# Moving a depthwise convolution from VectorE and GpSimd to TensorE, with half-size adaLN loads, in a two-layer hybrid attention and convolution backbone

## The reference

```python
for l in range(DEPTH):                        # DEPTH = 2
    mod   = silu(c) @ w_ada[l] + b_ada[l]     # six 1024-wide vectors (shift, scale, gate) x 2
    mod_c = silu(c_ctx) @ w_ada[l] + b_ada[l] # the same for the context
    h = modulate(rmsnorm(x, g_mix[l]), sh1, sc1)
    q, k, v, u = split_in(h @ w_in[l])        # 8 query heads, 2 key/value heads, u: 2 x 512
    a_out  = latent_attention(rope(q), rope(k), v, k_ctx, v_ctx, sink)
    cv_out = conv_module(u, ...)
    x = x + gt1 * merge_groups(a_out, cv_out, ...)   # rmsnorm of each, then @ w_out
    x = x + gt2 * swiglu(modulate(rmsnorm(x, g_ffn[l]), sh2, sc2))   # d_ff = 2816

def conv_module(u, w_dw, b_dw, ln_g, ln_b):   # w_dw: 31 taps x 512 channels
    z = u[..., :512] * sigmoid(u[..., 512:])
    z = depthwise_conv(z, w_dw, pad 15) + b_dw       # along the tokens, channel by channel
    return silu(layernorm(z, ln_g, ln_b))
```

## Time and profile before

| | |
|---|---|
| median of 3 runs | 1822.05 us (1820.49 to 1824.18) |
| profiled execution, first to last instruction | 1815.9 us |
| so outside the span, taken from the median | 6.15 us |
| PE busy | 1543.5 us (85%) |
| DVE busy | 1074.1 us (59%) |
| ACT busy | 630.1 us (35%) |
| POOL busy | 523.2 us (29%) |
| chain of work that ended last | PE 59%, DVE 25% of the span |
| HBM read | 146.71 MB |

### The profile page before, as it was taken

How to read it: one execution, slowest core, us unless ns; L and a number is a source line. 1 busy time by engine, 2 the same in 40 slices (tenths; PEclk the granted TensorE clock), 3 DMA queues, 4 the chain that set the end, 5 groups by cost and what they waited for, 6 DMA issues and landing times.

```text
span 1815.9 us, 24713 instructions
## 1 busy us (share of the span) xinstructions
PE 1543.5 (85%) x9388; PEld 1320.2 (73%) x9388; DVE 1074.1 (59%) x1612; ACT 630.1 (35%) x1002; POOL 523.2 (29%) x374
## 2 busy tenths in 40 slices
PE   4976636759889999999999999655778899999997
PEld 1765426647678887888788879654656898998995
DVE  2599999978644332334224356998877644444445
ACT  2310117984343411222112233114974453222222
POOL 0399999803300000000000003999913100000000
PEclk8988767989899999999999999877988999999998
DMA  8332300001111233213332252111001222223222
GB/s 346 115 127 97 135 24 12 1 1 36 39 55 58 89 138 134 68 58 104 141 114 59 95 206 70 47 35 35 1 1 58 82 92 93 92 88 92 93 84 84
DMA packets 35929, 149.80 MB, mean 82 GB/s; under 512 B 3984, under 2 KB 4368, under 8 KB 29712
## 3 DMA queue, kind: packets, MB, share of 16 engines
q1 hardware_dynamic: 35856, 148.82, 24.1%
HBM read 146.71 MB, written 2.10 MB: 82 GB/s over the span
## 4 chain that ended last, share of the span: by engine, by line
PE 59%; DVE 25%; issue 6%; ACT 5%; POOL 2%; DMA 2%; SPq 0%; DVEq 0%; ACTq 0%; POOLq 0%
PE banks L402 54%; DVE conv L1086 5%; DVE w_low L843 2%; POOL x L1296 2%; DVE probT L978 2%; PE banks L360 2%; DVE ssum L1079 2%; DVE row_max L942 1%; DMA ada_raw<-in_w_ada 1%; DVE psums L956 1%; DVE tmp L1020 1%; PE banks L494 1%; DVE sq L1017 1%; DVE tmp L887 1%; DVE q_stacked L1103 1%
## 5 line engine op out<-in xcount | busy, mean ns | idle before, releaser
L402 PE MATMUL banks<-h_high,w_high 128*128 128x258 f32 (+2 forms) x2048 | 510.7, 329 | 113.5 <-DVE w_low L843 83.5
L402 PE MATMUL banks<-h_low,w_high 128*128 128x258 f32 (+2 forms) x2048 | 498.3, 323 | 0.0
L402 PE MATMUL banks<-h_high,w_low 128*128 128x258 f32 (+2 forms) x2048 | 497.3, 322 | 0.0
L402 PEld LDWEIGHTS banks<-h_high,w_high 128*128 128x128 f32 x2048 | 330.2, 196 | 164.2 <-DVE w_low L843 81.1
L580 ACT ACTIVATE w_high<-raw 128x1024 fp32r<-128x1024 f32 (+1 forms) x178 | 185.1, 1040 | 626.9 <-PE banks L402 597.8
L843 DVE TENSOR_TENSOR w_low<-raw,w_high 128x1024 fp32r<-128x1024 f32 (+1 forms) x178 | 235.5, 1323 | 243.9 <-ACT w_high L580 240.7
L402 PEld LDWEIGHTS banks<-h_low,w_high 128*128 128x128 f32 x2048 | 330.6, 196 | 29.3 <-issue 0.7
L402 PEld LDWEIGHTS banks<-h_high,w_low 128*128 128x128 f32 x2048 | 327.1, 194 | 28.3
L1283 POOL TENSOR_TENSOR conv<-conv,diag_or_product 128x798 f32<-128x798 f32 (+1 forms) x160 | 269.7, 1685 | 13.3
L886 DVE COPY shift_product<-banks 128x2 f32<-128x2 f32 x116 | 18.4, 158 | 308.2 <-PE banks L402 294.3
L1281 POOL TENSOR_SCALAR diag_or_product<-z_padded,par 128x798 f32<-128x798 f32 (+1 forms) x160 | 179.7, 1123 | 15.7
(11 more groups left out here) (128 smaller groups left out, 1566.6 us busy)
## 6 DMA issues: line engine op xcount, KB each, us to landing
ada_raw<-in_w_ada SPq DMA_DIRECT2D x48, 1024.0 KB, 4.9
raw<-in_w_gu SPq DMA_DIRECT2D x88, 512.0 KB, 3.5
raw<-in_w_dn SPq DMA_DIRECT2D x32, 512.0 KB, 3.5
raw<-in_w_mix SPq DMA_DIRECT2D x28, 512.0 KB, 4.1
raw<-in_w_out SPq DMA_DIRECT2D x16, 512.0 KB, 3.5
raw<-in_w_dn SPq DMA_DIRECT2D x16, 384.0 KB, 3.1
x<-in_xT SPq DMA_DIRECT2D x8, 384.0 KB, 7.9
out_yT<-x SPq DMA_DIRECT2D x8, 256.0 KB, 2.2
```

Of the source, the lines that this page charges most:

```text
L402: last = mm(bank[:, 2 * slot + bk, 0:b - a], weights[w][:, k0_w + k, :], rhs[:, k0_rhs + k, a:b], start=(k == 0 and n == 0), stop=(k == kt ...
```

## The change

The convolution goes to PE. Its taps are padded to 32 and taken four at a time (TG = 8 groups). A 128-row operand is built for each quarter q of a channel tile: the 32 channels of the quarter four times over, each copy shifted by one more token. SP makes it with 16 DMAs a tile from `z` to `z_shifted` (`zr`), within the chip's own memory, each 32 partitions wide. `w_conv`, prepared on the host, holds for each tap group the four weights of each channel as 32-column matrices. A tile is 8 groups x 4 quarters x 2 column ranges (512 and, in layer 0, 256) in fp32. ACT copies the sum out with the bias (`conv_copy`). The taps of DVE and POOL go. The adaLN units are halved to 128 x 1024 (0.5 MB), 16 a group; group 0 has eight buffers of its own, the later groups keep two, now of half the size.

```diff
-ZW = PAD + N + 2 * PAD + L + PAD
-CC = N + 2 * PAD
-CVW = CC + L
+AHW = AGW // 2
+ADA_UNITS, EARLY = 2 * DT, 8
+CC = N + PAD
+ZW = PAD + N + PAD + L + PAD + 3
+SH = 4
+TG = -(-TAPS // SH)
+QC = P // SH
+RW = CC + L + SH * (TG - 1) + 2
...
-            return [(ADA_IN[layer, name], k) for k in range(DT) if k * (blocks - 1) // (DT - 1) == block]
...
+            return [(ADA_IN[layer, name], u) for u in range(ADA_UNITS) if u * (blocks - 1) // (ADA_UNITS - 1) == block]
+
+        Z_SHIFTS = {("u", 5): 0, ("u", 7): 1, ("qkv", 0): 2, ("qkv", 1): 3}
...
             def load_ada(unit):
-                i = unit[0] * DT + unit[1]
-                if i >= 2:
+                i = unit[0] * ADA_UNITS + unit[1]
+                tile, landed, _ = ada_buffer(i)
+                if EARLY <= i < ADA_UNITS:
+                    sp.wait_ge(ada_mm, i - EARLY + 1)
+                if i >= ADA_UNITS + 2:
                     sp.wait_ge(ada_mm, i - 1)
...
+            def shift_z(layer, k):
+
+                if k == 0:
+                    sp.wait_ge(zpad, layer + 1)
+                sp.wait_ge(z_ok, CT * layer + k + 1)
+                if k >= 2:
+                    sp.wait_ge(conv_mm, CT * layer + k - 1)
+                w = (CC + L if layer == 0 else N) + SH * (TG - 1)
+                for q in range(SH):
+                    for c in range(SH):
+                        sp.dma_start(zr[k % 2][QC * c:QC * c + QC, q, 0:w], z[QC * q:QC * q + QC, k, c:c + w])\
+                            .then_inc(zr_in[k % 2], 16)
+                if k >= 2:
+                    load_conv(layer, k)
...
-                    if (layer, name) in ADA_IN:
+                    if name in ("u", "qkv") or (layer, name) in ADA_IN:
+                        late = []
                         for i in range(pairs):
                             for j in range(2):
                                 if base + i > 0:
                                     sp.wait_ge(w_low, 2 * (base + i) + j - 1)
                                     load_block(i, j)
-                                for u in ada_units(layer, name, 2 * i + j):
+                                if (name, 2 * i + j) in Z_SHIFTS:
+                                    shift_z(layer, Z_SHIFTS[name, 2 * i + j])
+                                for u in late:
                                     load_ada(u)
+                                late = ada_units(layer, name, 2 * i + j)
+                        for u in late:
+                            load_ada(u)
                     else:
+                        if name == "oa" and layer + 1 < DEPTH:
+                            sp.wait_ge(conv_mm, CT * (layer + 1))
+                            for k in range(2):
+                                load_conv(layer + 1, k)
...
+            def conv_tile(layer, k):
...
+                n, j = CT * layer + k, k % 2
+                pe.wait_ge(wd_in[j], 16 * (n // 2 + 1))
+                pe.wait_ge(zr_in[j], 16 * SH * SH * (n // 2 + 1))
...
+                for g in range(TG):
+                    for bk, a, b in [(0, 0, N)] + ([(1, CC, CC + L)] if layer == 0 else []):
+                        for q in range(SH):
+                            last = mm(bank[QC * q:QC * q + QC, BC + bk, 0:b - a], wD[j][:, g, QC * q:QC * q + QC],
+                                      zr[j][:, q, SH * g + a:SH * g + b], start=(g == 0), stop=(g == TG - 1),
+                                      tile_position=(0, QC * q))
+                last.then_inc(conv_mm, 1)
...
                         for u in ada_units(layer, name, 2 * i + j):
                             ada_unit(u)
...
+                    if name == "u" and i:
+                        conv_tile(layer, i - 1)
...
+                        if i + j == 0:
+                            conv_tile(layer, CT - 1)
...
+            def conv_copy(layer, k, width):
+
+                act.wait_ge(conv_mm, CT * layer + k + 1)
+                f(cv[:, k, 0:width], wide[:, 512 * BC:512 * BC + width], ACT.Identity, bias=col("b_dw", k, layer))\
+                    .then_inc(conv_ok, 1)
```

More of the change, by code:

```diff
@@ L123, in hybrid_backbone @@
         wL = [sb(f"w_low{j}", [P, DT, P], F32R) for j in range(2)]
-        ada_raw = [sb(f"ada_raw{j}", [P, AGW]) for j in range(2)]
-        ssum = sb("ssum", [P, CVW])
+        ada_raw = [sb(f"ada_raw{j}", [P, AHW]) for j in range(2)]
+        wD = [sb(f"w_conv{j}", [P, TG, P]) for j in range(2)]
+        ssum = sb("ssum", [P, T])
         sq = [sb(f"sq{j}", [P, T]) for j in range(2)]
@@ L184, in hybrid_backbone @@
         ada_in = [sem(f"ada_in{j}") for j in range(2)]
+        early_in = [sem(f"ada_early_in{j}") for j in range(EARLY)]
+        wd_in = [sem(f"w_conv_in{j}") for j in range(2)]
+        zr_in = [sem(f"z_shifted_in{j}") for j in range(2)]
         y_out = sem("out_stored")
@@ L298, in load_ada, with load_conv @@
             def load_ada(unit):
-                i = unit[0] * DT + unit[1]
-                if i >= 2:
-                    sp.wait_ge(ada_mm, i - 1)
-                sp.dma_start(ada_raw[i % 2][:], w_ada[unit[0], unit[1]]).then_inc(ada_in[i % 2], 16)
-            for k in range(2):
-                load_ada((0, k))
+                i = unit[0] * ADA_UNITS + unit[1]
[3 more added lines that the diff above has]
+                if i >= ADA_UNITS + 2:
+                    sp.wait_ge(ada_mm, i - 1)
+                sp.dma_start(tile[:], w_ada[unit[0], unit[1]]).then_inc(landed, 16)
+            def load_conv(layer, k):
+                sp.dma_start(wD[k % 2][:].rearrange("p g m -> p (g m)"), w_conv[layer, k]).then_inc(wd_in[k % 2], 16)
+            def shift_z(layer, k):
[11 more added lines that the diff above has]
+                    load_conv(layer, k)
             for k in range(DT):
                 sp.dma_start(x[:, k, :], xT[k]).then_inc(x_in, 16)
-                if k % 2 and k < 5:
-                    load_ada((0, k // 2 + 2))
+                load_ada((0, k))
                 if k == 3:
@@ L354, in ada_unit @@
             def ada_unit(unit):
-                g, k = unit
-                i = g * DT + k
-                pe.wait_ge(ada_in[i % 2], 16 * (i // 2 + 1))
+                g, u = unit
+                half, k = u // DT, u % DT
+                tile, landed, count = ada_buffer(g * ADA_UNITS + u)
+                pe.wait_ge(landed, count)
                 for q in range(4):
-                    last = mm(bank[32 * q:32 * q + 32, ADA, :], cond[:, k, :], ada_raw[i % 2][:, 512 * q:512 * q + 512],
-                              start=(k == 0), stop=(k == DT - 1), tile_position=(0, 32 * q))
+                    last = mm(bank[32 * q:32 * q + 32, ADA, 256 * half:256 * half + 256], cond[:, k, :],
+                              tile[:, 256 * q:256 * q + 256], start=(k == 0), stop=(k == DT - 1), tile_position=(0, 32 * q))
                 last.then_inc(ada_mm, 1)
@@ L426, in phase @@
                     after[name == "u"].append((3, lambda: ada_turn(TURN_IN[layer, name])))
-                for i in range(pairs if with_ada else 1):
+                loop = not with_ada and name != "u"
+                for i in range(1 if loop else pairs):
                     for j in range(2):
@@ L716, in _ @@
                     last.then_inc(gate_ok, 1)
+                    if 0 < i < CT - 1:
+                        conv_copy(layer, i - 1, width)
                 ada_after(layer, "u")
+                conv_copy(layer, CT - 2, width)
                 for i in range(3):
@@ L732, in _ @@
                             last.then_inc(qk_high, 1)
+                            conv_copy(layer, CT - 1, width)
                         else:
@@ L1311, in weight_blocks, with conv_blocks @@
     return np.ascontiguousarray(blocks.reshape(layers, n // 2, 2, P, -1).transpose(0, 2, 1, 3, 4))
+def conv_blocks(w):
+    taps = np.zeros((DEPTH, TG * SH, CW), np.float32)
+    taps[:, 0:TAPS, :] = w
+    taps = taps.reshape(DEPTH, TG, SH, CT, SH, QC)
+    out = np.zeros((DEPTH, CT, SH, QC, TG, SH, QC), np.float32)
+    c = np.arange(QC)
+    out[:, :, :, c, :, :, c] = taps.transpose(5, 0, 3, 2, 1, 4)
+    return out.reshape(DEPTH, CT, P, TG * P)
 def host_constants():
@@ L1341 @@
     for l in range(DEPTH):
[L1342 removed]
+        table += [cols(a[n][l]) for n in ("b_ada", "g_mix", "g_ffn", "g_attn_out", "g_conv_out", "b_dw", "ln_g", "ln_b")]
         table.append(np.broadcast_to(a["attn_sink"][l][None, :], (P, HEADS)))
```

130 lines of the change are left out of this document (48 added, 82 removed).

## The result

| | before | after |
|---|---|---|
| median | 1822.69 us (4 runs beside those of after) | 1836.55 us (1832.99 to 1839.75, 4 runs) |
| ratio | | 1.0079, 95% interval 1.0064 to 1.0094 |
| profiled execution: span, time | 1815.9 | 1836.0, 1837.83 |

I predicted 1794; it is 43 us more, on the other side of no change and outside the range. Only 1.83 us lie outside the span of after (about 2.0 in the executions of before that are on record with the experiments); the rest of my 6.15 must come from before's profiled execution being shorter than the median. So the miss in the span is larger, 48 us (1836.0 against 1788), and 5 us of it are hidden by that term.

The account below looks back on a forecast made before the run. The prediction took DVE to bound `u` and `qkv` and PE the feed-forward phases. Its terms, -3.5 - 2.1 - 27.6 - 10 + 15.3 = -27.9, gave a span of 1788, with 6.15 outside it 1794 us; range 1758 to 1820.

Parts of the forecast that it names:

- my 6.15: Whole kernel: 6.15 us lie outside the profiled span, added to the forecast span of 1788 to give 1794.
- the sentence on cover: dn phases: loads queued on SP behind the copies are needed a block later; without cover, one 5 us late costs 5.
- four things that I named as signs of being wrong: Copies over 15 us a tile, a quarter waiting for another, three halves not stalling PE, a held SP load delaying `split_high`.
- Copies, 9.8 us a tile: Shifted copies on SP: 16 issues in 7.6 us, last landing 2.2 later, 9.8 in all; 6 to 18 kept.
- The term for its waits, 2 us each: Layer 0, u and qkv: PE waits 2 us for the copies of each of convolution tiles 0, 1 and 2.
- The rival "copies slow": Copies taking 18 us a tile make PE wait 8 more for four tiles, 32 in all: 1826; chance 0.10.
- the third-half stall: u, qkv and dn: with two buffers, PE stands 3.3 us for the third adaLN half behind one block.
- Start, -3.5: Start-up to the first gemm block: last rotary table lands at 35.3 instead of 38.85 us; range 0 to -5.
- Layer 0, -2.1: Layer 0, u and qkv to the first row maximum: PE becomes the bound, 225.5 us against 227.6.
- dn, +15.3: dn phases, three groups: 2.4 us for halves, 9.9 for three third-unit stalls, 3 for the clock.
- Layer 1, -27.6: Layer 1, second gemm block to first row maximum: 113.1 us against 140.7, with a wait of 3 for tile 0.
- Attention, -7 and -3: Attention without POOL's work: four-block units take 2.22 instead of 2.68 us; 7 saved in layer 0, 3 in layer 1.

Follow-up runs that it names:

- carry_and_pool: Changed kernel with copies issued by GpSimd and leftover half loads behind the next phase's first weight load, third halves left in: 1795.20 us, 0.9858 of before.
- all_three: Changed kernel with evenly placed halves, GpSimd copies, leftover halves behind next phase's first weight load, layer 1's first two `w_conv` loads ahead of `gu0`: 1768.54 us, 0.9716 of before.

## Why the prediction was wrong

*The step that failed* is the sentence on cover: "SP's queue behind the copies holds loads needed a block later". It was one of four things that I named as signs of being wrong; another was copies of over 15 us a tile, and both came. carry_and_pool is the changed kernel with the order of the queues mended, and with GpSimd's faster issue in the bargain (7.8 to 8.0 us a tile for 10.0 to 11.6). It takes 1795.2 us against my 1794: of the 43 us between forecast and result, 39 (by the ratios) to 41 (by the medians) go with the queues. That it lands 1 us from the forecast is luck in part: its span is 5.7 us over the 1788, and the rows below cancel. Parts:

- *Copies, 9.8 us a tile.* 15.8 in layer 0, 11.6 in layer 1. The bounds of 6 to 18 hold both. The term for its waits, 2 us each, became 7.85, 7.78 and 5.19, and each was followed by half clock in the tile (13.14 against 10.51).
- *What stands behind them.* I let SyncE be busy for 7.6 us a tile and moved nothing. It was busy for 10 to 11.6, and `w_conv` and the next block's weights came that much later.
- *Leftover halves, which I did not see.* `for u in late: load_ada(u)` at the end of a phase stands ahead of the next phase's first weight load, and a half's wait is for PE to come two halves further: 7.6 us at q0, 5.9 at layer 1's first block, 4 ahead of the attention. It is in the diff that I read. I costed the halves' loads where PE waits for them, not where something waits behind them. In the tail alone I had counted two halves ahead of the load.
- *The rival "copies slow"* said from 17 us a tile no gain; it counted only PE's waits. With the queue behind them 15.8 was enough.

*What held*, as to the mechanism and nearly the size: the third-half stall (3.3; the nine of after took 2.71 to 3.45); that quarters run together; the tile (10.5 and 7.1 for 11.2 and 7.2); layer 0's tail (23.4 us from q4 to the row maximum, 24.4 worked out); that DVE binds in layer 1's `rope` (7.55 for 7.35).

*What was mis-sized*, by carry_and_pool, where the sum agrees partly because errors cancel:

- *Start, -3.5.* -1.0. My 32.5 + 2.8 = 35.3 for the last table was 37.75. The loads run at 401 to 410 GB/s, not 415 (0.6 us), and the first five microseconds bring 167 GB/s, so that the start and the landing take some 4.6, not 2.8.
- *Layer 0, -2.1.* -13.0 once the queue is right: four tiles 0.7 cheaper, none of the three waits of 2, and at least 2 us that I can't place.
- *dn, +15.3.* +22.4. A stalling half costs 6.1 us (7.1 against 1.0 in `dn0`, carry_and_pool against all_three), not 4.3: the half clock and the loads behind it take 2.8, not 1.
- *Layer 1, -27.6.* -22.9. Tile 0 waits 4.5 us for 3 and then runs partly at half clock, 9.64 for 7.2; the four steps of the `rope` chain take 7.5 to 7.9 us for 7.3. From q0 to q1 it takes 12.9 us, as worked out (12.95); the 16.8 of the changed kernel are the queue again, 2.77 of them PE's wait for tile 3's `w_conv`.
- *Attention, -7 and -3.* -5.0 and -3.5 from the first row maximum to the last head unit. Behind layer 0's, 1.3 to 1.4 come back in both kernels up to the wait before `gu0`, which I have not explained; the rest to `gu0` differs by the clock alone (14.55 us in before, 15.36 in the changed kernel, 12.98 in carry_and_pool).

*Open:* why sixteen copies take 0.63 to 0.72 us each on SyncE and 0.49 on GpSimd. In layer 1, at two thirds of the bytes, they take as long on SyncE, so it isn't the bytes alone. And I did not try the change with whole units, or with a third adaLN buffer, so what the half size itself is worth beside the convolution is not shown.

## What to carry to other kernels

When a change adds waits to a queue, list what stands behind each one, phase ends included, and ask of every item when it is needed. Here a load that cost half a microsecond to issue held up a weight block that cost 4 to 7.6. An engine that a change has emptied is the first place for its new transfers. Work that comes in threes against two buffers stalls once in three: place it evenly.

## What the hardware showed

- Copies within the chip's memory, each out of 32 partitions, moved 155 to 211 GB/s when issued four a tile; sixteen a tile held SyncE for 10.0 to 11.6 us at 101.4 KB and at 67.5 KB alike, GpSimd for 7.8 to 8.0.
- The nine idle times of TensorE of 2.7 to 3.5 us for a third half were followed by 3.4 to 6.8 us at 1.2 GHz. After the same idle time of 2.92 us before `gu0` the changed kernel ran at 1.2 GHz in one execution and at 2.4 in another. In layer 0's stretch the mean clock was 0.88 with the waits and 0.96 without.
- Transfers issued behind another on the same queue did not make it land later: 37.94 us where 1 MB of `w_conv` was moved away from behind it and 1 MB of halves came at 34.05, against 37.54 to 38.07 with them right behind it.
